# The down product of a mixture-of-experts layer, turned: weights loaded in 32-column pieces for four column groups, token rows streamed, 32x32 block transposes after it

## The chip, the cores and the metric

The kernel runs on one core of a Trainium2 chip. The metric is the device time of one execution in microseconds; the kernel before takes 1264.74 us, the median of three runs.

## What is computed

One inference step of a two-layer decoder: layer 0 mixes tokens by latent attention, layer 1 by causal pooling, and each layer ends in the same kind of mixture of experts. 520 tokens (512 of a prompt, 8 samples) of width 1024 go to 2 of 16 experts each. The part that the change touches is the last line of this function:

```python
def moe(x, w_router, router_bias, w_gate, w_up, w_down):
    B, S, D = x.shape
    t = x.reshape(B * S, D)
    combine = route(t, w_router, router_bias).astype(x.dtype)
    h = jax.nn.silu(jnp.einsum('td,edf->tef', t, w_gate)) * jnp.einsum('td,edf->tef', t, w_up)
    y = jnp.einsum('tef,efd->td', h * combine[:, :, None], w_down)
    return y.reshape(B, S, D)
```

All data are float32. Per expert w_gate and w_up are 1024 x 512, w_down is 512 x 1024: three matrices of 2 MiB.

## The kernel before

All engines run hand-written streams that meet at semaphores. Router and tables sort the tokens by expert into the DRAM tensor `expert_rows` (`xs`), in tiles of `CAP` = 96 rows; a tile belongs to one expert. Here each layer has 16 tiles, so `nh` = 8 passes over a pair of tiles, s = 0 and 1. The result rows of a tile go to the DRAM tensor `expert_out` (`yd`); after the layer's last tile GpSimd (POOL) gathers each token's two rows from there by indirect DMA (L1012) and VectorE (DVE) adds them up with their weights.

A tile (`tl` = 2u + s) goes like this.

- **Weights.** SyncE (SP) issues one DMA for each of the three matrices (`load_expert`, L443, L447, L451) into one of two rings in SBUF. A matrix is loaded for the tile after the next as soon as TensorE is through with it in this tile: the DMAs wait for `gate_ps`, `up_ps` and `down_ps`.
- **Rows in.** ScalarE (ACT) issues four DMAs for the 96 token rows (`load_rows`, L1147), each into 32 partitions, 3 rows of 256 floats to a partition. This is done two tiles ahead, and the four DMAs stand in ACT's stream right behind the store of the tile before. DVE turns the rows with a 32x32 block transpose (`turn_rows`, L1586) into `xeT`, which holds the model width on partitions. In DVE's stream this transpose for the next tile stands between the gate product and the `h` products of this one.
- **Gate, up.** TensorE (PE) multiplies in two column groups (64 weight columns each, `at` = 0 and 64, so that two matmuls share the array), 128 matmuls of 96 streamed columns for each of gate (L851) and up (L861).
- **h.** ACT applies Silu to the gate (L1171), DVE multiplies with up (L1599 for the first three blocks of 128, L1602 for the last) into `h`, which has the expert width on partitions and the 96 rows along the free dimension.
- **Down.** PE takes `h` (128 x 96) as the weights and streams w_down, 512 columns at a time: 16 matmuls (L873) into PSUM banks 4 and 5, one result row to a partition.
- **Rows out.** ACT copies bank 4 (L1175) and DVE bank 5 (L1606) into `ys`; ACT then issues one DMA of 96 rows of 4 KB (L1177). Before writing `ys[s]` both wait for its earlier store (`y_st`).

ACT's stream for a tile is thus: issue the rows of tile tl + 2, Silu, copy bank 4, issue the store. SP's queue and ACT's queue are separate DMA queues that use the same 16 DMA engines.

The prediction names also: `h_set` (DVE tells PE that a part of h is there), `y_set` (banks copied out), `xe_ld` (rows landed), and L1627, DVE's first large step after the last tile of layer 0, which waits for `state_pool`. That is loaded by SP behind the first weights of layer 1.

Of the kernel before, what the change touches and what calls it, by code (L numbers as in the profile page):

```python
# [8 lines left out]
D = 1024  # L9
# [5 lines left out]
KD = D // P  # L15
# [8 lines left out]
KF = F // P  # L24
# [98 lines left out]
def build(nc, t, consts_shape, place):  # L123

    ctx = ExitStack()
    with ctx:
# [104 lines left out]
        ys = [view(arena, 5120 + 1024 * s, D) for s in range(2)]  # L231
# [135 lines left out]
        def _(sp):  # L367
# [87 lines left out]
            for L in range(2):  # L455
# [4 lines left out]
                else:  # L460
                    load_expert(1, 0, 1, (S[0]["gate_ps"][0], nh), (S[0]["up_ps"][0], 2 * nh), (S[0]["down_ps"][0], nh))
# [10 lines left out]
                    load_expert(1, 1, 0, (S[0]["gate_ps"][1], nh), (S[0]["up_ps"][1], 2 * nh), (S[0]["down_ps"][1], nh))  # L472
                sp.wait_ge(tab_set, 2 * L + 2)
                nh = sp.value_load(n_half[0:1, 0:1], min_val=E // 2, max_val=TILES // 2)
                with sp.Fori(1, nh) as u:
                    for s in range(2):
                        ex = sp.value_load(tile_ids[0:1, bass.ds(2 * u + s, 1)], min_val=0, max_val=E - 1)
                        load_expert(L, ex, 1 - s, (q["gate_ps"][s], u), (q["up_ps"][s], 2 * u), (q["down_ps"][s], u))
# [10 lines left out]
        def _(pe):  # L489
# [349 lines left out]
            def experts(L):  # L839
                q = S[L]  # L840

                def tile(u, s):
# [25 lines left out]
                    for blocks in (range(KF - 1), (KF - 1,)):  # L868
                        if KF - 1 in blocks:
                            pe.wait_ge(q["h_set"], 2 * tl + 2)  # L870
                        for hf in range(2):
                            for f in blocks:
                                last = nc.tensor.matmul(bank(4 + hf)[0:CAP, :], h[s][:, f, :], wd[w][:, f, 512 * hf:512 * (hf + 1)],  # L873
                                                        start=(f == 0), stop=(f == KF - 1))
                    last.then_inc(q["down_ps"][s], 1)
# [53 lines left out]
        def _(pool_e):  # L929
# [54 lines left out]
            for L in range(2):  # L984
# [19 lines left out]
                for s in range(2):  # L1004
                    hold(pool_e, q["y_st"][s], 16 * nh)
# [25 lines left out]
        def _(act):  # L1031
# [109 lines left out]
            def experts(L):  # L1141
# [13 lines left out]
                act.sem_inc(q["y_set"], 1)  # L1155

# [7 lines left out]
                def tile(u, s, stored):  # L1164
# [14 lines left out]
                tile(0, 0, False)  # L1179
                tile(0, 1, False)  # L1180
                with act.Fori(1, nh) as u:
                    tile(u, 0, True)
# [497 lines left out]
```

## Time and profile before

| | us |
|---|---|
| median of 3 runs (1263.69 to 1266.37) | 1264.74 |
| the profiled execution | 1262.56 |
| its span, first to last instruction | 1260.8 |
| PE busy, of the span | 1068.2 (85%) |
| DVE busy | 378.2 (30%) |
| ACT busy | 200.1 (16%) |
| expert stage of layer 0, first gate to last down product | 500.3 to 786.3 |
| expert stage of layer 1 | 915.9 to 1201.8 |

The span falls into the attention layer (to 500), 16 tiles, the pooling layer with its router (786 to 916), 16 tiles, and the last normalisation. PE is busy in the profile's sense whenever a matmul is in flight, which doesn't say that it runs at its peak. The granted clock is a share of PE's full clock: 1.00 is 2.4 GHz, 0.50 is 1.2 GHz. The DMA share is the mean busy share of the 16 DMA engines; records can overlap, so it can stand a little above 1.

### The profile page before, as it was taken

To read this page: it belongs to the slowest core of one execution; us is meant where nothing else is said; L and a number is where in the kernel's file an instruction comes from. 1 tells how busy PE (TensorE), PEld (TensorE's weight loads), DVE (VectorE), ACT (ScalarE), POOL (GpSimd) and SP (SyncE) were. 2 spreads that over 40 slices of the span, in tenths; PEclk is the share of its full clock that TensorE was granted. 3 is DMA by queue.
4 is the path that set the end of the run, shared out by engine and by line. 5 is a ranking of instruction groups with operands and counts; after the bars stand their busy time and mean duration, and the time that the engine had idled before them with its cause. 6 is when DMAs were issued, how large, how long until landed. Compare 5 with 4: busy or idle time off the path is not lost.

```text
span 1260.8 us, 27022 instructions
## 1 busy us (share of the span) xinstructions
PE 1068.2 (85%) x11219; PEld 763.1 (61%) x11219; DVE 378.2 (30%) x792; ACT 200.1 (16%) x433; POOL 122.4 (10%) x189
## 2 busy tenths in 40 slices
PE   7899999899999961999999999198099999999910
PEld 6678878545544411777777776187077777777700
DVE  1334444233233233111111111694421111111155
ACT  1234444300222101000000000121020000000011
POOL 0001011120033003000000000430300000000042
PEclk9989999999799975999999999587599999999965
DMA  9324245110023186999999999424479999999541
GB/s 341 138 73 149 80 144 185 56 48 1 1 75 90 53 354 232 325 380 392 392 390 389 399 396 354 157 70 168 151 250 390 384 387 392 402 394 390 202 163 52
DMA packets 80859, 295.96 MB, mean 235 GB/s; under 512 B 10184, under 2 KB 41168, under 8 KB 72495
## 3 DMA queue, kind: packets, MB, share of 16 engines
q1 hardware_dynamic: 53351, 247.50, 52.5%
q10 hardware_dynamic: 19712, 26.75, 6.2%
q0 software_dynamic: 7760, 21.24, 5.1%
q8 instruction: 22, 0.36, 0.1%
q14 instruction: 14, 0.11, 0.0%
HBM read 255.80 MB, written 40.11 MB: 235 GB/s over the span
## 4 chain that ended last, share of the span: by engine, by line
PE 83%; DVE 7%; DMA 3%; POOL 2%; issue 2%; ACT 2%; ACTq 0%; SPq 0%; POOLq 0%; DVEq 0%
PE PS L873 18%; PE PS L851 14%; PE PS L861 13%; PE PS L781 6%; PE PS L569 4%; PE PS L730 4%; PE PS L631 3%; PE PS L616 3%; PE PS L753 2%; PE PS L711 2%; PE PS L786 2%; PE PS L525 2%; PE PS L827 2%; PE PS L547 2%; POOL expert_rows L992 1%
## 5 line engine op out<-in xcount | busy, mean ns | idle before, releaser
L873 PE MATMUL PS<-ring,arena 128*96 128x512 f32 x512 | 227.4, 597 | 0.0
L851 PE MATMUL PS<-arena,ring 128*64 128x96 f32 x4096 | 179.3, 249 | 51.7 <-DVE arena L1586 51.7
L851 PEld LDWEIGHTS PS<-arena,ring 128*64 128x64 f32 x4096 | 173.3, 139 | 75.7 <-issue 75.7
L861 PE MATMUL PS<-arena,ring 128*64 128x96 f32 x4096 | 174.7, 246 | 0.2 <-issue 0.2
L861 PEld LDWEIGHTS PS<-arena,ring 128*64 128x64 f32 x4096 | 171.0, 137 | 0.4 <-issue 0.4
L873 PEld LDWEIGHTS PS<-ring,arena 128*96 128x96 f32 x512 | 80.8, 163 | 123.0 <-issue 119.2
L1586 DVE STREAM_TRANSPOSE arena<-arena 128x768 uint32<-128x768 uint32 x34 | 54.2, 1593 | 205.4 <-ACT arena L1171 175.5
L1606 DVE COPY arena<-PS 96x512 f32<-96x512 f32 x32 | 22.0, 687 | 218.0 <-PE PS L873 218.0
L1175 ACT ACTIVATE arena<-PS 96x512 f32<-96x512 f32 x32 | 19.0, 593 | 379.8 <-PE PS L873 379.8
L1012 POOL DMA_INDIRECT arena<-expert_out,ids x20 | 20.2, 1012 | 599.0 <-DMA expert_out<-arena 589.0
L781 PE MATMUL PS<-ring,arena 128*128 128x512 f32 (+1 forms) x160 | 75.8, 636 | 1.3 <-issue 0.7
L781 PEld LDWEIGHTS PS<-ring,arena 128*128 128x128 f32 (+1 forms) x160 | 28.4, 179 | 45.7 <-issue 45.0
L958 POOL DMA_DIRECT2D ring<-cache_krope x64 | 34.6, 541 | 152.4 <-issue 152.4
L569 PE MATMUL PS<-arena,ring 128*128 128x260 f32 x192 | 47.6, 400 | 1.0 <-POOL ring L936 0.7
L730 PE MATMUL PS<-ring,arena 128*16 128x512 f32 x96 | 44.7, 617 | 2.3 <-ACT arena L1193 2.1
L631 PE MATMUL PS<-ring 128*128 (+1 forms) x320 | 43.4, 271 | 2.0 <-ACT ring L1083 1.6
L800 PE MATMUL PS<-C,X 128*128 128x128 f32 x64 | 17.0, 386 | 31.3 <-POOL X L970 31.3
L631 PEld LDWEIGHTS PS<-ring 128*128 128x128 f32 x320 | 40.1, 191 | 4.6 <-issue 2.3
L569 PEld LDWEIGHTS PS<-arena,ring 128*128 128x128 f32 x192 | 36.9, 199 | 6.6 <-POOL ring L936 0.9
L616 PE MATMUL PS<-ring 128*128 128x512 f32 (+3 forms) x128 | 38.3, 442 | 2.2 <-ACT ring L1070 1.2
L1171 ACT ACTIVATE arena<-PS 128x384 f32<-128x384 f32 x32 | 15.7, 491 | 149.8 <-PE PS L851 149.8
L1078 ACT ACTIVATE ring<-PS,small 128x512 f32<-128x512 f32 (+1 forms) x64 | 33.0, 527 | 25.2 <-DVE small L1330 25.2
(225 smaller groups left out, 1059.7 us busy)
## 6 DMA issues: line engine op xcount, KB each, us to landing
ring<-w_gate SPq DMA_DIRECT2D x32, 2048.0 KB, 14.6
ring<-w_up SPq DMA_DIRECT2D x32, 2048.0 KB, 15.3
ring<-w_down SPq DMA_DIRECT2D x32, 2048.0 KB, 15.7
arena<-expert_rows ACTq DMA_DIRECT2D x144, 96.0 KB, 9.7
expert_out<-arena ACTq DMA_DIRECT2D x32, 384.0 KB, 7.8
expert_rows<-ring SPq DMA_DIRECT2D x6, 1920.0 KB, 10.0
ring<-cache_ckv SPq DMA_DIRECT2D x64, 128.0 KB, 2.0
ring<-w_o SPq DMA_DIRECT2D x1, 4096.0 KB, 19.1
```

What stands on the lines that cost most here:

```text
L525: last = nc.tensor.matmul(bank(n % 4, HALF), wdq[:, k, P * m:P * (m + 1)], XT[:, k, HALF * hf:HALF * (hf + 1)], start=(k == 0), stop=(k == ...
L569: last = nc.tensor.matmul(bank(b, HALF), wuq[:, m, P * parity:P * (parity + 1)], cq[:, m, HALF * hf:HALF * (hf + 1)], start=(m == 0), stop ...
L616: nc.tensor.matmul(score(i), qT[par][:, P * i:P * (i + 1)], kT[par][:, 0:P * (i + 1)], start=True, stop=True).then_inc(s_ps, 1)
L631: last = nc.tensor.matmul(bank(3, 4, VH, off=256 * par)[:, i, :], probT[:, i % 2, P * k:P * (k + 1)], V[:, k, bass.ds(P * p + VH * par, VH ...
L730: nc.tensor.matmul(bank(hf)[0:H, :], qb[s][:, c, :], kpT[:, c, 512 * hf:512 * (hf + 1)], start=(c == 0), stop=(c == 2))
L781: last = nc.tensor.matmul(bank(b0 + hf)[0:n, :], oT[:, k, P * i:P * i + n], wo[:, k, 512 * hf:512 * (hf + 1)], start=(k == 0), stop=(k == ...
L851: last = nc.tensor.matmul(bank(s, KF, CAP)[at:at + 64, f, :], wg[w][:, k, P * f + at:P * f + at + 64], xeT[s][:, k, :], start=(k == 0), st ...
L861: last = nc.tensor.matmul(out[at:at + 64, :], wu[w][:, k, P * f + at:P * f + at + 64], xeT[s][:, k, :], start=(k == 0), stop=(k == KD - 1))
L873: last = nc.tensor.matmul(bank(4 + hf)[0:CAP, :], h[s][:, f, :], wd[w][:, f, 512 * hf:512 * (hf + 1)], start=(f == 0), stop=(f == KF - 1))
L958: pool_e.dma_start(krp[s][:, n, 0, :], t["cache_krope"][0, bass.ds(page, 1), :, :].rearrange("a p d -> (a p) d")).then_inc(kr_ld, 16)
L1078: nc.scalar.activation(prob[:, i, 0:P * (i + 1)], score(i), ACT.Exp, scale=-1.0, bias=mneg[:, c:c + 1], accum_out=rsum[:, c:c + 1]).then_i ...
L1586: v.transpose(xeT[s].rearrange("p m (a j) -> p a m j", j=32).bitcast(mybir.dt.uint32), xe[s].rearrange("p a (i m) -> p a m i", i=32).bitca ...
```

## The change

The down product changes sides. w_down is now the loaded operand: 32 neighbouring columns for each of four column groups, which take columns 256c + 32m for c = 0 to 3; `h` is streamed, 96 columns. That makes 8 x 4 x 4 = 128 matmuls for a tile in place of 16. The result stands turned, output columns on partitions: DVE puts it back with two 32x32 block transposes out of PSUM, which replace both copies. `ys` then has the layout of `xe`, 32 partitions for each quarter of the width, and the store becomes four DMAs with pieces of 256 floats (1 KB). ACT has no copy left. `down_ps` counts twice a tile, `y_st` to 64.

```diff
-        ys = [view(arena, 5120 + 1024 * s, D) for s in range(2)]
+        ys = [view(arena, 5120 + 1024 * s, CAP // 32, D // 4) for s in range(2)]
...
-                        load_expert(L, ex, 1 - s, (q["gate_ps"][s], u), (q["up_ps"][s], 2 * u), (q["down_ps"][s], u))
+                        load_expert(L, ex, 1 - s, (q["gate_ps"][s], u), (q["up_ps"][s], 2 * u), (q["down_ps"][s], 2 * u))
...
-                    for blocks in (range(KF - 1), (KF - 1,)):
-                        if KF - 1 in blocks:
-                            pe.wait_ge(q["h_set"], 2 * tl + 2)
-                        for hf in range(2):
-                            for f in blocks:
-                                last = nc.tensor.matmul(bank(4 + hf)[0:CAP, :], h[s][:, f, :], wd[w][:, f, 512 * hf:512 * (hf + 1)],
-                                                        start=(f == 0), stop=(f == KF - 1))
-                    last.then_inc(q["down_ps"][s], 1)
+
+                    def down(m, blocks):
+                        for f in blocks:
+                            for c in range(4):
+                                last = nc.tensor.matmul(bank(4 + m // 4, 4, CAP)[32 * c:32 * c + 32, m % 4, :],
+                                                        wd[w][:, f, 256 * c + 32 * m:256 * c + 32 * m + 32],
+                                                        h[s][:, f, :], start=(f == 0), stop=(f == KF - 1))
+                        return last
+
+                    down(0, range(KF - 1))
+                    down(4, range(KF - 1))
+                    pe.wait_ge(q["h_set"], 2 * tl + 2)
+                    down(0, (KF - 1,))
+                    down(4, (KF - 1,))
+                    for m in (1, 2, 3, 5, 6, 7):
+                        last = down(m, range(KF))
+                        if m in (3, 7):
+                            last.then_inc(q["down_ps"][s], 1)
...
-                    act.wait_ge(q["down_ps"][s], u + 1)
-                    if stored:
-                        act.wait_ge(q["y_st"][s], 16 * u)
-                    nc.scalar.activation(ys[s][0:CAP, 0:512], bank(4)[0:CAP, :], ACT.Copy).then_inc(q["y_set"], 1)
                     act.wait_ge(q["y_set"], 2 * tl + 4)
-                    act.dma_start(yd[bass.ds(CAP * tl, CAP), :], ys[s][0:CAP, :]).then_inc(q["y_st"][s], 16)
...
+                    for c in range(4):
+                        act.dma_start(yd[bass.ds(CAP * tl, CAP), 256 * c:256 * (c + 1)].rearrange("(a j) d -> j a d", j=32),
+                                      ys[s][32 * c:32 * (c + 1), :, :]).then_inc(q["y_st"][s], 16)
...
-                    dve.wait_ge(q["down_ps"][s], u + 1)
                     if stored:
-                        dve.wait_ge(q["y_st"][s], 16 * u)
-                    v.tensor_copy(ys[s][0:CAP, 512:D], bank(5)[0:CAP, :]).then_inc(q["y_set"], 1)
+                        dve.wait_ge(q["y_st"][s], 64 * u)
+                    for g in range(2):
+                        dve.wait_ge(q["down_ps"][s], 2 * u + g + 1)
+                        v.transpose(ys[s].rearrange("p a (m i) -> p a m i", m=KD)[:, :, 4 * g:4 * g + 4, :].bitcast(mybir.dt.uint32),
+                                    bank(4 + g, 4, CAP).rearrange("p m (a j) -> p a m j", j=32).bitcast(mybir.dt.uint32)
+                                    ).then_inc(q["y_set"], 1)
```

In ACT's stream, one tile of the loop over pairs, before (from the rows-in DMAs on; ISA rows compute an address or wait):

```order
L1147 DMA arena<-expert_rows 32x3x256
L1170 REGISTER_ALU
L1171 ACTIVATE arena<-PS 128x384 [waits gate_ps0_0]
L1174 REGISTER_ALU [waits down_ps0_0]
L1175 ACTIVATE arena<-PS 96x512 [waits y_st0_0]
L1176 ISA
L1177 ISA [waits y_set_0]
L1177 DMA expert_out<-arena 96x1024
L1147 ISA [waits xeT_set_0]
L1147 DMA arena<-expert_rows 32x3x256
```

The same piece of ACT's stream now:

```order
L1157 DMA arena<-expert_rows 32x3x256
L1178 REGISTER_ALU
L1179 ACT_TABLE_LOAD
L1179 ACTIVATE arena<-PS 128x384 [waits gate_ps0_0]
L1180 ISA
L1182 ISA [waits y_set_0]
L1182 DMA expert_out<-arena 32x3x256
L1182 ISA
L1182 DMA expert_out<-arena 32x3x256
L1182 ISA
L1182 DMA expert_out<-arena 32x3x256
L1182 ISA
L1182 DMA expert_out<-arena 32x3x256
```

The copy and its waits are gone; four DMAs with the shape of the rows-in DMAs stand where one stood, ahead of the next tile's rows. A load of the activation table stands in the loop, ahead of the wait for the gate product.

In DVE's stream, one tile of the loop, now:

```order
L1600 ISA [waits sg_set_0]
L1590 STREAM_TRANSPOSE arena<-arena 128x3x8x32 [waits xe_ld1_0]
L1603 TENSOR_TENSOR arena<-arena,PS 128x288 [waits up_ps0_0]
L1605 REGISTER_ALU
L1606 TENSOR_TENSOR arena<-arena,PS 128x96 [waits up_ps0_0]
L1608 REGISTER_ALU
L1611 STREAM_TRANSPOSE arena<-PS 128x3x128 [waits down_ps0_0,y_st0_0]
L1611 STREAM_TRANSPOSE arena<-PS 128x3x128 [waits down_ps0_0]
```

The order of the steps is as before; the two transposes out of PSUM stand where the copy of bank 5 stood. The turn of the next tile's rows still stands ahead of both h products.

## Rows read from the trace of the kernel before

**Rows 1.** The page's part 5: line, engine, operation, shapes, count; busy us, mean ns.
```profile
L873 PE MATMUL PS<-ring,arena 128*96 128x512 f32 x512 | 227.4, 597 | 0.0
...
L1586 DVE STREAM_TRANSPOSE arena<-arena 128x768 uint32<-128x768 uint32 x34 | 54.2, 1593 | 205.4 <-ACT arena L1171 175.5
```

**Rows 2.** The chain that ended last, one tile of layer 0: start us, us.
```profile
619.55 7.04 PE PS L873 x16
626.59 5.43 PE PS L851 x128
632.02 5.28 PE PS L861 x128
```

**Rows 3.** The same chain, layer 1: its first gate product, last down product, last store.
```profile
915.89 7.35 PE PS L851 x128
...
1194.74 7.05 PE PS L873 x16
1202.68 3.04 DMA expert_out<-arena
```

**Rows 4.** A window in layer 0's tiles: busy by engine, granted clock, DMA share, GB/s.
```profile
572.00:750.00 178.00, 178.00 (x2723) 131.41 (x2722) 29.93 (x40) 10.85 (x20) 0.00 (x0) 1.00 1.02 392
```

**Rows 5.** Loads of w_down issued from 500 to 540 us: issue to landing.
```profile
DMA to landing us min/median/max: 12.2/12.6/12.9
```

**Rows 6.** Loads of w_down issued from 1120 to 1170 us: issue to landing.
```profile
DMA to landing us min/median/max: 16.4/16.5/16.5
```

**Rows 7.** Timeline of SP's DMA issues, the last of layer 1.
```profile
1166.32 0.38 SPq L451 DMA_DIRECT2D ring<-w_down  x1
```

**Rows 8.** The page's part 3: SP's queue (q1), ACT's (q10): packets, MB, share.
```profile
q1 hardware_dynamic: 53351, 247.50, 52.5%
q10 hardware_dynamic: 19712, 26.75, 6.2%
```

**Rows 9.** The page's part 6: ACT's two kinds of DMA: count, KB each, us to landing.
```profile
arena<-expert_rows ACTq DMA_DIRECT2D x144, 96.0 KB, 9.7
expert_out<-arena ACTq DMA_DIRECT2D x32, 384.0 KB, 7.8
```

**Rows 10.** Timeline of ACT, 655 to 692 us, behind the down product ending at 662.1.
```profile
663.08 0.36 ACTq L1177 DMA_DIRECT2D expert_out<-arena  x1
663.63 1.77 ACTq L1147 DMA_DIRECT2D arena<-expert_rows  x4
```

**Rows 11.** Loads of expert_rows issued from 640 to 700 us: issue to landing.
```profile
DMA to landing us min/median/max: 8.4/10.1/12.1
```

**Rows 12.** Timeline of DVE, 655 to 692 us.
```profile
662.22 0.69 DVE L1606 COPY arena<-PS 96x512 f32<-96x512 f32 x1 [6.87 <-PE PS L873]
...
672.85 0.26 DVE L1602 TENSOR_TENSOR arena<-arena,PS 128x96 f32<-128x96 f32 x1 [0.87 <-PE PS L861]
...
685.93 1.59 DVE L1586 STREAM_TRANSPOSE arena<-arena 128x768 uint32<-128x768 uint32 x1 [5.38 <-ACT arena L1171]
```

**Rows 13.** Timeline around the router's last part, layer 0: PE and its weight loads.
```profile
465.37 1.02 PE L503 MATMUL PS<-C,X 8*128 8x8 f32 x8 [5.64 <-DVE X L1453]
...
466.67 0.47 PEld L827 LDWEIGHTS PS<-wr,ring 128*8 128x8 f32 x16 [0.38 <-ACT ring L1121]
466.67 0.59 PE L827 MATMUL PS<-wr,ring 128*8 128x16 f32 x16 [0.29 <-ACT ring L1121]
```

**Rows 14.** The window around it; columns as in rows 4.
```profile
465.00:470.00 5.00, 1.61 (x24) 1.40 (x24) 2.01 (x8) 1.92 (x4) 0.00 (x0) 0.50 1.01 429
```

**Rows 15.** Windows of 3 us within one tile; columns as in rows 4.
```profile
663.90:666.90 3.00, 3.00 (x78) 3.00 (x76) 0.00 (x0) 0.00 (x0) 0.00 (x0) 1.00 1.02 434
...
669.80:672.80 3.00, 3.00 (x75) 2.88 (x70) 0.46 (x1) 0.00 (x0) 0.00 (x0) 1.00 1.05 342
```

**Rows 16.** Timeline behind layer 0's last tile, whose down product ended at 786.3 us.
```profile
787.76 1.28 ACT L1126 ACT_TABLE_LOAD   x1 [0.80 <-DVE arena L1606]
...
790.88 2.29 DVE L1627 TENSOR_TENSOR arena<-arena 128x2048 f32<-128x2048 f32 x1 [3.69 <-DMA arena<-state_pool]
```

More of the change, by code:

```diff
@@ L460, in _ @@
                 else:
-                    load_expert(1, 0, 1, (S[0]["gate_ps"][0], nh), (S[0]["up_ps"][0], 2 * nh), (S[0]["down_ps"][0], nh))
+                    load_expert(1, 0, 1, (S[0]["gate_ps"][0], nh), (S[0]["up_ps"][0], 2 * nh), (S[0]["down_ps"][0], 2 * nh))
                     sp.wait_ge(S[0]["xeT_set"], 2 * nh + 1)
@@ L470, in _ @@
                     sp.dma_start(t["o_pool_s"][0, :, CTX - 1, :], X[0:DB, 4, :]).then_inc(pool_out, 16)
-                    load_expert(1, 1, 0, (S[0]["gate_ps"][1], nh), (S[0]["up_ps"][1], 2 * nh), (S[0]["down_ps"][1], nh))
+                    load_expert(1, 1, 0, (S[0]["gate_ps"][1], nh), (S[0]["up_ps"][1], 2 * nh), (S[0]["down_ps"][1], 2 * nh))
                 sp.wait_ge(tab_set, 2 * L + 2)
@@ L1004, in _ @@
                 for s in range(2):
-                    hold(pool_e, q["y_st"][s], 16 * nh)
+                    hold(pool_e, q["y_st"][s], 64 * nh)
                 def gather(i):
@@ L1154, in experts @@
                 nh = act.value_load(n_half[0:1, 0:1], min_val=E // 2, max_val=TILES // 2)
-                act.sem_inc(q["y_set"], 1)
                 act.wait_ge(scat, 160 * (L + 1))
@@ L1162, in experts, with tile @@
                     nc.scalar.activation(X[0:n, i, :], X[0:n, i, :], ACT.Copy, scale=ALPHA).then_inc(xscaled, 1)
-                def tile(u, s, stored):
+                def tile(u, s):
                     tl = 2 * u + s
@@ L1171, in tile @@
                     nc.scalar.activation(sg[s], bank(s, KF, CAP), ACT.Silu).then_inc(q["sg_set"], 1)
-                    act.wait_ge(q["down_ps"][s], u + 1)
-                    if stored:
-                        act.wait_ge(q["y_st"][s], 16 * u)
-                    nc.scalar.activation(ys[s][0:CAP, 0:512], bank(4)[0:CAP, :], ACT.Copy).then_inc(q["y_set"], 1)
                     act.wait_ge(q["y_set"], 2 * tl + 4)
-                    act.dma_start(yd[bass.ds(CAP * tl, CAP), :], ys[s][0:CAP, :]).then_inc(q["y_st"][s], 16)
[L1179 to L1182, printed above, removed]
-                    tile(u, 1, True)
+                    for c in range(4):
+                        act.dma_start(yd[bass.ds(CAP * tl, CAP), 256 * c:256 * (c + 1)].rearrange("(a j) d -> j a d", j=32),
+                                      ys[s][32 * c:32 * (c + 1), :, :]).then_inc(q["y_st"][s], 16)
+                with act.Fori(0, nh) as u:
+                    tile(u, 0)
+                    tile(u, 1)
             def take_pages(b):
@@ L1582, in experts @@
                 nh = dve.value_load(n_half[0:1, 0:1], min_val=E // 2, max_val=TILES // 2)
-                dve.sem_inc(q["y_set"], 1)
+                dve.sem_inc(q["y_set"], 2)
                 def turn_rows(s):
```

## The prediction

> **What bounds the kernel now.** I read the chain of waits first. In an expert stage it is TensorE alone: a tile takes 7.04 us of down product, 5.43 of gate and 5.28 of up [rows 2], 17.75 us from one down product to the next, 16 tiles in each of two layers, 32 in all. PE waits for nothing between tiles. Seen from PE alone, every microsecond off the down product is worth 32.
>
> The DMA view says otherwise. While PE sets the pace, the DMA engines' share is 1.02 at 392 GB/s [rows 4]. A tile needs three matrices of 2,097,152 bytes, four row loads of 98,304 and a store of 393,216, in all 7.08 MB, and 7.08 MB at 392 GB/s is 18.0 us, a bit more than the 17.75 that PE gives. That the loads fall behind shows in their landing: w_down takes 12.6 us early in layer 0 [rows 5] and 16.5 late in layer 1 [rows 6]. PE doesn't notice, for two whole tiles are in the rings when a stage begins. So the kernel is bound by PE, with the DMA engines full right behind it.
>
> The third view is ACT's queue. It has 19,712 packets [rows 8]. Its 144 row loads and 32 stores [rows 9] are 176 DMAs; with 96 pieces and 16 completions each that is 176 x 112 = 19,712, so completions count as packets. A tile's row loads and store are 5 x 112 = 560 packets. SP's matrices have 128, 128 and 512 pieces (16 KB, 16 KB, 4 KB) and 48 completions: 816. The store is issued at 663.08 and the four row loads up to 665.4 [rows 10]; the last has landed by 665.4 + 12.1 = 677.5 [rows 11]. ACT's 560 packets thus took 14.4 us at most, 39 or more per us; SP's 816 in 17.75 us are 46 per us. The counts per time are alike, though SP's packets are many times larger. I read this as **turns**: a DMA engine takes one packet from each queue in turn, whatever its size. The Trainium skill, DMA: Bandwidth & Descriptors, section Queues, rings and completion order, says that each engine goes round robin over the queues at packet granularity; it speaks of several descriptors to a packet, which no row here shows.
>
> **Down product.** 16 matmuls of 597 ns (they overlap, so that 16 take 7.04 us) [rows 1, 2] go; 128 with 32 columns loaded and 96 streamed come. No row has this form. From one side: the gate and up products stream the same 96 columns, 128 matmuls in 5.28 us, 41.3 ns each and 82.5 for a pair of column groups. If four groups fit in the time of two, a matmul costs 20.6 ns and a tile 2.6 us. From the other: if there is no more overlap than now, 41.3 ns and 5.3 us. Narrow weights are issued fast: 16 loads of 8 columns in 0.47 us, 29 ns each [rows 13], at a granted clock of 0.50 [rows 14]. I take 27 ns, near that row: **3.4 us**. PE's tile is then 5.43 + 5.28 + 3.4 = 14.1 us. The second wait for h is covered: DVE begins L1602 as up ends and takes 0.26 us [rows 12], and 24 matmuls at 27 ns stand ahead of the wait, 0.65 us. The rule of the Trainium skill that speaks against the change is in TensorE: Matmul & The Clock Gate, section Wait — 56ns, not 53.3ns?: about 62 ns per matmul where the sequencer decodes in software, 7.9 us for 128, which would make this product dearer than before. The 41.3 ns of rows 2 disagree with it; its other floor, 25 ns, would give 3.2 us.
>
> **Copies.** ACT's 0.59 us copy goes. DVE's goes too (0.69), and two transposes of 128 x 384 come. L1586 takes 1.59 us for 128 x 768 [rows 1], so I put 0.80 on each; reading PSUM might add a little. The first lies beside the down product, the second is exposed only before the store: +0.1 us. DVE is 30% busy. ACT's table load is now in the loop, 8 times a layer, 1.28 us each [rows 16]. It stands ahead of the wait for the gate product: after the store and row issues ACT is free about 5.5 us into the gate product of 5.4, so Silu comes late by half a us at worst, and L1599 still waits for up.
>
> **Store.** One DMA of 4 KB pieces becomes four of 1 KB pieces. Issue: three more at 0.36 us [rows 10], +1.1. Bytes are the same. Engine time: ACT's queue used 6.2% of 16 engines for 26.75 MB, 46.8 us per MB; SP's 42.8 [rows 8]. If only the row loads are dearer (14.16 MB), they cost 50.3, and the store at that price is 7.5 x 0.393 / 16 = +0.18 us a tile. That is the lower bound, and I take it. The upper: while row loads and w_down are in flight the rate falls from 434 to 342 GB/s [rows 15]; if the store does that for another 6 us, it costs 21% of 6, +1.25 us a tile. Nothing argues for a gain.
>
> **Turns.** This is the costly part. The store has 4 x 112 packets, ACT's queue 896 a tile, SP's still 816. Turn by turn, 896 take 896/46 = **19.5 us**, longer than PE's 14.1 and than the 18.0 of the bytes. Who waits: the rows of tile n+3 stand behind the store of tile n. They are there at most 15.4 us after n's down product ended at 662.1 [rows 10 to 12], and are turned at 685.9, 23.8 us after, one period and 6.1. Now they come 1.2 us later (issue) and 336/46 = 7.3 us later (turns): 23.9. Needed they are after 14.1 + 6.1 = 20.2 us while PE runs free, after 18.0 + 6.1 = 24.1 if the bytes bound. So they are late as soon as PE has sped up, and since each tile adds 1.5 us to the queue, they stay late. DVE stands at L1586 for them, with both h products behind it, and PE waits between up and down, 19.5 - 14.1 = 5.4 us. After an idle of 5.64 us the clock row shows 0.50, that is 1.2 GHz [rows 13, 14], and a first gate product after idle took 7.35 for 5.43 [rows 3]; I put nothing on these 1.9 us since PE has 5.4 to spare.
>
> **Sum, per layer.** Tiles 0 to 2 have their rows early and the last waits for none: 4 x (14.1 - 17.75) = -14.6. Twelve at 19.5: +21.0. SP's loads meanwhile run ahead (18.0 against 19.5, after three fast tiles); when both rings are full its queue empties, ACT's pieces go without taking turns, and a tile runs at 14.1. I count one such: -5.4. Net +1.0. The end: second transpose and issue, +1.2. Two layers: 2 x 2.2 = +4.4. The profiled execution, 1262.56 (span 1260.8), becomes 1267.0; it lies 2.2 below the median shown, and against that I say **1269.1**. With none or two such tiles per layer: 1280 or 1258.
>
> **Rivals.**
> A, ends faster: turns don't bind, rows arrive in time, the bytes bound the stage. w_down of the last tile is issued at 1166.32 [rows 7] and lands 16.5 later, 1182.8; the loads are full from early on, so it can't come much sooner. Add 14 x 0.18 = 2.6 and a down product of 3.4: 1188.8 against 1194.74 + 7.05 = 1201.8, -13.0 per layer. Ends +2.4; behind layer 0 `state_pool` (now used 4.6 us after the last product [rows 16]) queues behind more of layer 1's weights, +4.5. Sum -26.0 + 6.9 = -19.1: **1246**, give or take 6. For it: the 24.1 against 23.9 above; it decides if the queue takes under 18.0 us for its packets, that is 50 per us. Against: rows 10 and 11.
> B: the store disturbs the loads by 1.25 us a tile, 28 tiles: +35, **1304**. For it the dip [rows 15]; against, the dip needs writes into 32 partitions, and a store reads there.
> C: four groups don't overlap at all, 82.5 x 128 = 10.6 us; 3.5 x 32 = +113, **1378**. It decides from 55 ns a matmul (7.04/128). Against: two groups overlap now.
> D: the DMA engines have room (the rate is only what PE asks) and rows come in time: -3.65 x 32 = -117, plus 2.4 for the ends, **1150**. Against: the landings that grow.
>
> **Chances.** Forecast 0.60, A 0.26, B 0.08, C 0.03, D 0.03. 0.2% is 2.5 us, about what can be told from no change here. Of the forecast's 0.60, which spreads over 1258 to 1280, 0.13 lies faster, 0.12 within, 0.35 slower. Faster: 0.13 + 0.26 + 0.03 = 0.42; same 0.12; slower 0.35 + 0.08 + 0.03 = 0.46. The range takes in most of A and the first part of B's price: 1243 to 1287; D, C and most of B are left out. The forecast's own is 1258 to 1280.
>
> **What would show it.** Right: the down product in 2.6 to 5.3 us; idle time before it, or before h, put down to row loads; row loads landing 20 us and more after issue, up from 10; ACT's queue at 272 x 112 = 30,464 packets; dips of the granted clock inside the stages; a few tiles near 14 us, the others over 18. Wrong: row loads landing within 18 us and PE waiting for the ring's loads instead (A); a down product over 7 us (C); matrices landing later and later with rows in time (B); no waits at all (D).

## The result, and the profile after

The changed kernel takes **1494.21 us** (median of 4 runs, 1483.13 to 1498.01), against 1265.55 for the kernel before (1263.69 to 1272.49): ratio 1.178, 95% interval 1.170 to 1.186. The prediction was 1269.1, from 1243 to 1287. The sign is the likelier one (slower had 0.46), the size is wrong: 229 us more, where the forecast had 4, and none of the cases had the cause.

The page after, the lines that answer to rows 1, 8 and 9:

```profile
span 1496.3 us, 42722 instructions
...
PE 1101.0 (74%) x18899; PEld 919.4 (61%) x18899; DVE 393.6 (26%) x824; ACT 199.0 (13%) x415; POOL 121.5 (8%) x189
...
q1 hardware_dynamic: 53351, 247.50, 45.7%
q10 hardware_dynamic: 30464, 26.76, 6.1%
...
q8 instruction: 162, 2.65, 0.7%
...
L851 PE MATMUL PS<-arena,ring 128*64 128x96 f32 x4096 | 226.5, 281 | 145.3 <-issue 93.3
...
L872 PE MATMUL PS<-arena,ring 128*32 128x96 f32 x8192 | 207.9, 261 | 104.4 <-issue 104.4
...
L1611 DVE STREAM_TRANSPOSE arena<-PS 128x384 uint32<-128x384 uint32 x64 | 37.3, 583 | 283.4 <-PE PS L872 283.4
...
arena<-expert_rows ACTq DMA_DIRECT2D x144, 96.0 KB, 5.9
```

The same two lines of the page before:

```profile
q8 instruction: 22, 0.36, 0.1%
...
L851 PE MATMUL PS<-arena,ring 128*64 128x96 f32 x4096 | 179.3, 249 | 51.7 <-DVE arena L1586 51.7
```

Three things stand out. PE now has idle time put down to **issue**: it waited for no other engine and no transfer that the profile can name. Queue q8, which brings instructions, has 162 packets where it had 22. And the row loads, which the prediction saw as the late ones, land in 5.9 us, sooner than before [rows 9]. The waits of PE, with total, times and longest:

```profile
PE PS L872 <- issue: 104.4, 51, 3.9
PE PS L851 <- issue: 93.3, 29, 5.2
PE PS L851 <- DVE arena L1590: 52.0, 2, 26.1
PE PS L861 <- issue: 5.1, 5, 1.3
```

The 52.0 are the start of the two stages and were there before. The other three make 203 us, new. The chain that ended last shows where they lie; two tiles of layer 0, to be held against rows 2:

```profile
596.93 3.45 issue
600.38 7.40 PE PS L851 x128
607.78 5.28 PE PS L861 x128
613.07 2.61 PE PS L872 x119
615.67 1.41 issue
617.08 2.84 PE PS L872 x128
619.92 2.26 issue
622.19 0.41 PE PS L872 x9
622.59 5.43 PE PS L851 x128
628.02 5.28 PE PS L861 x128
633.30 2.60 PE PS L872 x117
635.90 3.70 issue
639.60 5.35 PE PS L872 x128
644.95 0.03 issue
644.97 0.66 PE PS L872 x11
645.63 3.43 issue
649.07 7.02 PE PS L851 x127
```

PE stops **every 128 matmuls** (a few less where waits and register instructions stand between them). Each matmul record comes with a weight load (8192 of each for L872), so 128 matmuls are 256 instruction records. q8 moved 2.65 MB in 162 packets, 16.4 KB each, so one packet is 64 bytes for each of 256 records. The 140 packets more are 8.75 for each of the 16 passes of the loop, and a pass has 2048 records (2 tiles of 512 matmuls and 512 loads) besides waits and registers, 8 packets' worth. I read this so, and the runs below test it: after each block of 256 records PE has nothing to issue until the next block has come, and the whole body is brought anew in every pass. In the gate and up products 128 matmuls last 5.3 us and the gap is mostly covered; in the down product they last 2.6 to 2.8 and it is not.

The blocks don't lie alike in the two layers. In layer 0 seven stops stand at the gate product, one for each backward branch (23.1 us). In layer 1 there are 22: seven at the branch, seven more 13 matmuls behind it, the rest in the pass's second tile. One of layer 1's passes, right behind the branch:

```profile
1123.43 1.38 PE PS L851 x13
1124.81 4.33 issue
```

Near the end of layer 1, when the last weights have landed (DMA share 0.03 from 1414.6 to 1420.0), the whole down product of 256 matmuls runs without a stop:

```profile
1414.59 5.45 PE PS L872 x256
```

The second part is the clock, in windows of the same stretch (columns as in rows 4):

```profile
600.00:604.00 4.00, 3.62 (x46) 3.62 (x48) 0.00 (x0) 1.28 (x1) 0.00 (x0) 0.50 1.03 386
...
622.00:628.00 6.00, 5.81 (x141) 5.67 (x142) 0.58 (x1) 0.00 (x0) 0.00 (x0) 1.00 0.70 231
...
640.00:645.00 5.00, 4.97 (x128) 4.62 (x120) 0.58 (x1) 0.00 (x0) 0.00 (x0) 0.50 0.54 225
```

After an idle of 3.45 or 3.70 us the granted clock is 0.50 (1.2 GHz), and 128 matmuls of the down product take 5.35 us for 2.84; after 2.26 us it is still 1.00. These two tiles take 649.07 - 600.38 = 48.7 us, before 35.5. Of the 13.2 more, issue is 10.8, the low clock 5.8 (the products' 37.9 against 2 x (5.43 + 5.28 + 5.34) = 32.1; the 256 matmuls of a down product at full clock take the 5.34 that 128 of them take at 0.50), and the cheaper down product gives back 3.4. Over the layers, first gate to last down product: 386.7 us (502.5 to 889.2) and 418.7 (1018.2 to 1437.0), against 286.0 and 285.9. That is 233.5 of the 235.5 us between the spans.

The loop over 320 us of layer 0 (560 to 880):

```profile
560.00:880.00 320.00, 246.74 (x6766) 236.30 (x6762) 47.11 (x67) 14.08 (x19) 0.00 (x0) 0.89 0.80 291
```

The DMA engines are no longer full (0.80 for 1.02 [rows 4]), so neither turns nor bytes can be what binds here.

### The profile page after: what moved, and what is told of

Its sections match the earlier page's. It is cut to its first block, busy times and chain, and to the rows that moved or that the text cites. A ratio compares the mean times of both kernels' runs of the same rounds, so it can differ in the third digit from the quotient of the medians.

```text
span 1496.3 us, 42722 instructions
## 1 busy us (share of the span) xinstructions
PE 1101.0 (74%) x18899; PEld 919.4 (61%) x18899; DVE 393.6 (26%) x824; ACT 199.0 (13%) x415; POOL 121.5 (8%) x189
## 3 DMA queue, kind: packets, MB, share of 16 engines
q10 hardware_dynamic: 30464, 26.76, 6.1%
q8 instruction: 162, 2.65, 0.7%
## 4 chain that ended last, share of the span: by engine, by line
PE 72%; issue 15%; DVE 6%; DMA 3%; POOL 2%; ACT 2%; ACTq 0%; SPq 0%; POOLq 0%; DVEq 0%
PE PS L851 15%; PE PS L872 14%; PE PS L861 11%; PE PS L781 5%; PE PS L569 3%; PE PS L730 3%; PE PS L631 3%; PE PS L616 2%; PE PS L753 2%; PE PS L525 2%; PE PS L711 2%; PE PS L786 1%; PE PS L827 1%; PE PS L547 1%; POOL expert_rows L1002 1%
## 5 line engine op out<-in xcount | busy, mean ns | idle before, releaser
L851 PE MATMUL PS<-arena,ring 128*64 128x96 f32 x4096 | 226.5, 281 | 145.3 <-issue 93.3
L851 PEld LDWEIGHTS PS<-arena,ring 128*64 128x64 f32 x4096 | 218.1, 164 | 154.2 <-issue 152.3
L872 PE MATMUL PS<-arena,ring 128*32 128x96 f32 x8192 | 207.9, 261 | 104.4 <-issue 104.4
L872 PEld LDWEIGHTS PS<-arena,ring 128*32 128x32 f32 x8192 | 189.8, 117 | 118.7 <-issue 115.0
L861 PE MATMUL PS<-arena,ring 128*64 128x96 f32 x4096 | 178.4, 246 | 5.2 <-issue 5.1
L861 PEld LDWEIGHTS PS<-arena,ring 128*64 128x64 f32 x4096 | 173.3, 137 | 6.9 <-issue 6.5
L1611 DVE STREAM_TRANSPOSE arena<-PS 128x384 uint32<-128x384 uint32 x64 | 37.3, 583 | 283.4 <-PE PS L872 283.4
```

The source lines that it names most:

```text
L851: last = nc.tensor.matmul(bank(s, KF, CAP)[at:at + 64, f, :], wg[w][:, k, P * f + at:P * f + at + 64], xeT[s][:, k, :], start=(k == 0), st ...
L861: last = nc.tensor.matmul(out[at:at + 64, :], wu[w][:, k, P * f + at:P * f + at + 64], xeT[s][:, k, :], start=(k == 0), stop=(k == KD - 1))
L872: last = nc.tensor.matmul(bank(4 + m // 4, 4, CAP)[32 * c:32 * c + 32, m % 4, :], wd[w][:, f, 256 * c + 32 * m:256 * c + 32 * m + 32], h[s ...
L1611: v.transpose(ys[s].rearrange("p a (m i) -> p a m i", m=KD)[:, :, 4 * g:4 * g + 4, :].bitcast(mybir.dt.uint32), bank(4 + g, 4, CAP).rearra ...
```

## The experiments

Theory F (fetch): the loop body of PE has outgrown what stays loaded, and the dense down product uses up instructions faster than they come. Rivals: the form with four column groups is slow in itself; the store's small pieces (turns, as predicted); a backward branch alone. The kernel before, run beside them, had medians of 1264.7 (runs 1 to 4), 1262.0 (5 to 8) and 1263.6 (9 to 12). Edits are against the changed kernel unless said otherwise; of the longer ones only the lines that carry the change are shown, and they shift the line numbers, so that the down product stands at L872, L873 or L874. Runs 4 to 8 and run 12 have one execution each, the others 4 to 10.

**1. Two column groups** instead of four: half the instructions for the same result. The columns are taken 8 apart, and DVE's transposes write them 8 apart too. Body 1536 records.

```diff
+                        n = 4 if False else 2
...
-                            for c in range(4):
-                                last = nc.tensor.matmul(bank(4 + m // 4, 4, CAP)[32 * c:32 * c + 32, m % 4, :],
-                                                        wd[w][:, f, 256 * c + 32 * m:256 * c + 32 * m + 32],
...
+                            for c in range(n):
+                                cols = wd[w][:, f, D // n * c:D // n * (c + 1)].rearrange("p (i m) -> p i m", m=KD)[:, :, m]
+                                last = nc.tensor.matmul(bank(4 + m // 4, 4, CAP)[P // n * c:P // n * (c + 1), m % 4, :],
```

> The changed kernel, but with two column groups of 64 in place of four of 32 (columns 8i + m of a half, which the second transpose puts back): 64 matmuls of the program a tile for the down product, not 128, and a PE loop body of 1536 matmul and load records in place of 2048. Theory F (the loop body is larger than what TensorE's sequencer keeps, so its code is loaded anew in every pass, behind the weights in the DMA queues): the instruction queue falls from 162 packets to about 22 as before, the idle time put down to issue inside the expert stages goes, the down product stays near 5.3 us, and the time is 1225 to 1275 us. Rival G (four column groups or the turned form are slow in themselves, by drains between forms): the drains stay, since gate, up and down are still turned products, and the time stays above 1350. Rival T (ACT's queue with 896 packets a tile bounds the stage): row loads land late and DVE waits for them, 19.5 us a tile, 1265 to 1320 us.

Measured: **1284.6** us, ratio 1.014 (1.009 to 1.019). q8 has 25 packets, and of the issue waits in the tiles 0.2 us is left. 209.6 us are gone, and still the time lies over the 1225 to 1275 that theory F had. Besides the number of instructions and of groups only the order of the columns is new, and run 4 takes that by itself. What is left over the kernel before is something else: 64 columns that lie 8 apart load slowly (218 ns a load; 140 dense, L851), and the down product takes 7.76 us, more than the 7.04 it replaced.

```profile
L874 PEld LDWEIGHTS PS<-arena,ring 128*64 128x64 f32 x4096 | 252.5, 218 | 3.9 <-issue 3.9
```

**2. The kernel before, with four tiles instead of two in a pass** (against the kernel before). Every instruction is the same; body 2176 records.

```diff
-                with pe.Fori(0, nh) as u:
-                    for s in range(2):
-                        tile(u, s)
+                with pe.Fori(0, E // 4) as v4:
+                    for d in range(2):
+                        for s in range(2):
+                            tile(2 * v4 + d, s)
```

> The kernel before, with four tiles in place of two in a pass of TensorE's loop (and a fixed number of passes): the same matmuls in the same order, but a body of 2176 records where it had 1088. Theory F: code is loaded again in each of the 8 passes, about 9 packets each, so the instruction queue goes from 22 packets to about 90, and there is idle time put down to issue; since the down product of 512 columns gives 7 us for few records, much of it can be hidden: 10 to 80 us slower. Rivals G and T: no change, within 3 us of the kernel before.

Measured: **1291.0** us, ratio 1.020 (1.015 to 1.025), q8 90 packets. The waits appear without any turned product:

```profile
PE PS L851 <- issue: 11.5, 12, 2.6
PE PS L861 <- issue: 8.3, 8, 1.5
```

They are 20 us and not 200. There are half as many blocks (38 packets in each stage, against 71 and 78 in the change), and the 16 long matmuls of a down product last 7 us for 32 records, in which I take it that the next block comes.

**3. The kernel before with only its store split** into four DMAs of 1 KB pieces (against the kernel before): the prediction's turns by themselves.

```diff
-                    act.dma_start(yd[bass.ds(CAP * tl, CAP), :], ys[s][0:CAP, :]).then_inc(q["y_st"][s], 16)
+                    for c in range(4):
+                        act.dma_start(yd[bass.ds(CAP * tl, CAP), 256 * c:256 * (c + 1)], ys[s][0:CAP, 256 * c:256 * (c + 1)]
+                                      ).then_inc(q["y_st"][s], 16)
```

> The kernel before, with the store of a tile's result as four DMAs of 96 pieces of 1 KB in place of one with 96 of 4 KB: ACT's queue has 896 packets a tile in place of 560, nothing else is changed. Theory T: 896 packets at 46 per us take 19.5 us where a tile has 17.75; row loads land some 7 us later, and after a few tiles DVE waits for them: 10 to 50 us slower. Theory F alone: no change, row loads later but in time, within 5 us.

Measured: **1277.8** us, ratio 1.010 (1.006 to 1.013). Row loads land in 18.7 us instead of 9.7, DVE waits for them, and PE from there for h (16 waits, 16.1 us in all):

```profile
DVE arena L1588 <- DMA arena<-expert_rows: 240.9, 28, 15.2
```

A stage takes 294.4 and 295.4 us, 18.4 a tile. The waits are there as forecast, for +13 us; it can't be what costs 229.

**4. Four groups, columns 8 apart**: the stride of run 1 in the form of the change.

```diff
+                        n = 4 if True else 2
...
-                                                        wd[w][:, f, 256 * c + 32 * m:256 * c + 32 * m + 32],
...
+                                cols = wd[w][:, f, D // n * c:D // n * (c + 1)].rearrange("p (i m) -> p i m", m=KD)[:, :, m]
```

> The changed kernel with four column groups as it is, but the same column order as in the run with two groups (columns 8i + m of each quarter, read with a stride of 32 bytes): the control for the stride. Theory F: as the changed kernel, about 160 instruction packets and 1470 to 1510 us, if a strided load of 32 columns costs what a dense one does. If the stride makes the loads dearer, the down product's busy time grows beyond 5.4 us a tile and the time with it.

Measured: 1495.6 us, q8 162, issue waits 99.2 + 95.3 + 7.1. The stride lengthens a load of 32 columns (143 ns for 117) and costs no time beside the stops. So runs 5, 6 and 12, which mix both group counts and need it, can be read against the change.

**5, 6 and 12. Smaller bodies**, by taking the first of the eight m with four groups and the rest with two, with the columns 8 apart as in runs 1 and 4:

```diff
+                        n = 4 if m < 5 else 2
-                            for c in range(4):
+                            for c in range(n):
```

(m < 7 gives 1984 records, m < 5 gives 1856, m < 2 gives 1664.)

> Four column groups for seven of the eight column positions m and two groups for the last: 120 down matmuls of the program a tile in place of 128, so TensorE's loop body has 1984 matmul and load records, 3% fewer than the 2048 of the changed kernel, and otherwise the same work. Theory F, code is kept if the whole body fits in 2048 records: the instruction queue falls to about 25 packets and the time to 1250 to 1290 us. If the limit is in whole blocks of 256 records and the body lies across nine of them: still about 160 packets and 1450 to 1500 us. If the number of records doesn't matter but the form of four groups does: 1450 us or more with few packets.

> As the run before, with four groups for five of the eight positions and two for three: a body of 1856 records, 7.25 blocks of 256. Theory F: it lies across eight or nine blocks; about 25 packets and 1255 to 1295 us if eight are kept, about 160 packets and over 1400 us if it happens to touch nine. Down product about 5 x 0.67 + 3 x 0.97 = 6.2 us a tile.

> Four column groups for m = 0 and 1, two for the rest (strided columns as in the run with two groups): body of PE's loop 1664 records, between 1536 (q8 25, no issue waits, 1284.6) and 1856 (q8 154, 137 us of issue waits, 1441.5). If a loop is kept only up to some size that lies between 1664 and 1856, q8 stays near 25 and the time is near 1284. If the limit lies between 1536 and 1664, q8 is near 130 packets (6.5 of 256 records a pass, 16 passes, and the 22 of the rest) and issue waits come back, of some 100 us: 1380 to 1420. A middle case, q8 around 50 and waits of 20 us, would say that the kept part shrinks gradually.

| body, records | q8 packets | issue waits in the tiles, us | time, us |
|---|---|---|---|
| 2048 (the change) | 162 | 203 | 1494.2 |
| 1984 | 162 | 190 | 1514.6 |
| 1856 | 154 | 137 | 1441.5 |
| 1664 | 26 | 2 | 1298.5 |
| 1536 (run 1) | 25 | 0.2 | 1284.6 |

It is a **step, and it lies between 1664 and 1856 records**. At 1664 the mix of both forms of matmul runs without a gap:

```profile
602.92 5.28 PE PS L861 x128
608.20 8.19 PE PS L874 x160
616.38 5.28 PE PS L851 x128
```

So four groups don't leave gaps by themselves; and that they aren't slow in themselves the change's own chain says, with 119 of its matmuls in 2.61 us. Above the step q8 has no middle value: everything is fetched in each pass, not only what doesn't fit (at 1856 each stage of 8 passes has 70 packets). The 14 us between 1664 and 1536 are the down product's 8.19 us for 7.76. At 1984 the waits are a little fewer, yet the time is 20 us longer, and over the 1450 to 1500 expected for a body across nine blocks; its two-group part loads slowly, and I leave the rest open.

**7. PE's loop unrolled**, so that no branch goes back.

```diff
-                with pe.Fori(0, nh) as u:
+                for u in range(E // 2):
```

> The changed kernel with TensorE's loop over the 8 pairs written out as straight code, so that no branch goes back. Theory F, with code arriving about every 5 us a block of 256 records behind the weight traffic: the records used are the same, 64 blocks a layer, so it stalls about as much, 1400 to 1500 us, with 150 or more packets. Rival, the backward branch is what defeats the fetching ahead: 1250 to 1320 us with as many packets.

Measured: **1421.5** us, q8 141.

```profile
PE PS L872 <- issue: 139.0, 59, 3.9
PE PS L851 <- issue: 7.4, 3, 3.1
```

Of the 93 us of waits at the gate product 86 are gone, but not all of them were the branch's. In the change the 14 stops right at the branch make 46.6 us (one is the 3.43 at 645.63), those 13 matmuls behind it, in layer 1, another 31.5, and 15.3 stand in the second tile of a pass, where only a block ends. The waits inside the down product stay, and grow by 35. In all 149.5 of 203 us are left: straight code streams too slowly as well, and that is the greater part.

The Trainium skill, Runtime: NRT & Kernel Launch, section Instruction fetch mechanics, describes blocks of 16 KiB or 256 instructions, and a stall after a taken branch whose target is outside a window of two pages. The size agrees with the packets here (16.4 KB, 128 matmuls apart). The stops at the branch agree with the stall, but the window does not: the kernel before goes back over 1088 records, more than four blocks, and has no such stop. The Trainium skill also says, in the same section, that crossing a block is mostly hidden, because an engine issues more slowly than blocks arrive. Here PE issued 256 records in 2.6 to 2.8 us, and the trace disagrees, with gaps of 1.4 to 3.9 us. And the Trainium skill gives PE, in the same section, room for 2048 instructions. That is eight blocks, and the runs leave it open: at 1856 records a pass has 8.75 packets, since waits and registers come on top of the records and a loop need not begin where a block does.

**8. Less weight traffic.** From a layer's third tile on, the loads bring an eighth of w_gate and w_up and a quarter of w_down; PE's instructions are all there, and it multiplies with what older weights stand in the ring for the rest. The DMA share in the tiles falls to 0.38 and 0.33.

```diff
-                sp.dma_start(wg[s], t["w_gate"][L, bass.ds(e, 1), :, :].rearrange("a (p k) f -> p (a k) f", p=P)
+                sp.dma_start(wg[s][:, 0:n, :], t["w_gate"][L, bass.ds(e, 1), :, :].rearrange("a (p k) f -> p (a k) f", p=P)[:, 0:n, :]
```

> The changed kernel with only an eighth of each gate and up matrix and a quarter of each down matrix loaded from the third tile of a layer on; the rest of a matrix is what stood in the ring, so the outputs are not the reference's. TensorE's program is the same, 160 instruction packets. Theory F, a code packet waits behind weight packets in the 16 DMA engines: the waits put down to issue shrink from 203 us to under 80 and the time to 1200 to 1350 us. Rival, the fetch takes its time by itself whatever else the DMA engines do: the waits stay near 200 us and the time near 1490 us.

Measured: 1335.5 us, q8 162 as in the change.

```profile
PE PS L852 <- issue: 66.3, 29, 3.7
PE PS L873 <- issue: 13.4, 18, 2.8
```

(L852 is the gate and L873 the down product here.) The same blocks come over the same DMA engines. With these a third busy, the stalls inside the down product shrink from 104 us to 13. Of the 93 at the gate product 66 stay, and they divide: the 14 stops at the branch take 48.3 us for 46.6, those 13 matmuls behind it 14.2 for 31.5, the others 3.8 for 15.3. So a block of instructions **waits behind the weights**, and that is most of what PE loses in straight code; the stop at the branch itself, 3.3 to 3.5 us, doesn't shrink with the traffic.

**9. Two groups of 64 neighbouring columns** (512c + 64m), so that loads are dense. The result's columns then stand in another order, and the two sums at the end take them by halves.

```diff
+                            for c in range(2):
+                                last = nc.tensor.matmul(bank(4 + m // 4, 4, CAP)[64 * c:64 * c + 64, m % 4, :],
+                                                        wd[w][:, f, 512 * c + 64 * m:512 * c + 64 * m + 64],
```

> The turned product with two column groups of 64 neighbouring columns each (columns 512c + 64m), so that weights are loaded dense; the columns of a row of expert_out stand in another order, and the last step's sums undo that with halves. Body of PE's loop: 1536 records. Fetch theory: q8 stays near 25 packets, no issue waits in the loop, granted clock as before; the down product costs what a gate product costs, 5.3 us a tile, PE's tile 16.0. Then the ACT queue's 896 packets a tile (18.3 to 18.5 us a tile in the run with the split store alone) or the bytes (18.0) set the stage: 1258 to 1280. If the strided loads were all that cost in the first two-group run (7.8 against 5.3 us, while PE had no idle time to give), it should come out below that run's 1284.6. If it is 1290 or more, something other than fetch and stride is slow in the turned product. If it is under 1240, neither turns nor bytes bind.

Measured: **1273.9** us, ratio 1.009 (1.006 to 1.012). The down product takes 5.28 us at full clock, but PE isn't what sets the pace; it waits for h 23 times, 51.2 us in all. The down products of the chain begin at 633.73 and 672.07 with row loads ahead of them:

```profile
DVE arena L1597 <- DMA arena<-expert_rows: 283.3, 28, 15.3
```

A stage takes 293.7 and 290.9 us, the pace of run 3 (18.4 a tile) or a little under it, though run 3's down product was the old one. PE has become faster by 1.8 us a tile and next to none of it arrives.

**10. The same with the stores issued from POOL's queue**, so that ACT's queue has only the rows.

```diff
+                        hold(pool_e, q["y_set"], 2 * tl + 4)
+                        for c in range(4):
+                            pool_e.dma_start(yd[bass.ds(CAP * tl, CAP), 512 * (c % 2) + 256 * (c // 2):512 * (c % 2) + 256 * (c // 2) + 256].rearrange("(a j) d -> j a d", j=32),
+                                             ys[s][32 * c:32 * (c + 1), :, :]).then_inc(q["y_st"][s], 16)
```

> As e9, but the four store DMAs of a tile are issued from POOL's queue, so that ACT's queue has the row loads alone (448 packets a tile) and the stores take turns of their own. Turns theory (a queue with more packets a tile than SP's 816 sets the pace): row loads land in about 10 us again and the stage goes at the bytes' 17.8 to 18.0 a tile, some 10 to 15 us under e9: about 1250, with 1240 to 1262 as limits. If the bytes or PE bound e9, nothing changes (within 4 us of e9). If the small store pieces disturb the weight loads wherever they are issued from, it is not faster than e9 either, and w_down lands later than 17 us.

Measured: **1257.1** us, ratio 0.9948 (0.9927 to 0.9969): faster than the kernel before, by half a per cent. Median landings, run 9 and then this run:

```profile
ring<-w_down SPq DMA_DIRECT2D x32, 2048.0 KB, 13.2
arena<-expert_rows ACTq DMA_DIRECT2D x144, 96.0 KB, 20.1
```

```profile
ring<-w_down SPq DMA_DIRECT2D x32, 2048.0 KB, 26.0
arena<-expert_rows ACTq DMA_DIRECT2D x144, 96.0 KB, 9.8
```

Two things differ, the queue of the stores (POOL's is q0, software_dynamic in the page) and, with it, the place of the rows: ACT no longer waits for `y_set` ahead of them, and issues them 8 us before the down product ends (612.08 for 620.0), where run 9 does it 3 us after (608.60 for 605.5). Run 11 has this early place with the stores still in ACT's queue. The rows land after half the time, the weights 13 us later, and PE now waits for weights, a little at a time (15.5 us for w_down, 11.1 for w_up). The stage takes 277.1 and 277.6 us, 17.3 a tile, but that is a mean of two paces. In each stage five or six tiles in a row go at 15.8, which is PE alone (three times 5.28). The last six go at 18.5:

```profile
682.15 5.50 PE L872 MATMUL PS<-arena,ring 128*64 128x96 f32 x128 [1.28 <-DMA ring<-w_down]
700.65 5.50 PE L872 MATMUL PS<-arena,ring 128*64 128x96 f32 x128 [0.90 <-DMA ring<-w_down]
```

Run 9's tiles go at 18.5 (layer 1: 18.4) from the second on, and in both runs the DMA engines are full; windows of run 9 and run 10, columns as in rows 4:

```profile
560.00:760.00 200.00, 181.38 (x4207) 179.92 (x4209) 34.97 (x55) 13.10 (x17) 0.00 (x0) 0.97 1.02 382
560.00:760.00 200.00, 188.41 (x4486) 185.49 (x4484) 40.43 (x58) 13.59 (x18) 24.66 (x46) 1.00 1.02 387
```

So the queue doesn't change what the DMA engines get done, it changes **who waits**. In run 9 the rows are late while weights lie ready (they land after 13.2 us); in run 10 PE first uses up the two tiles of weights in the rings at its own pace, and then takes the pace of the DMA engines. That is where the 13 to 17 us a stage come from. Between the stages 5.5 us are lost again (135.1 for 129.6), where `state_pool` takes 25.3 us.

**11. As run 9, the rows issued right behind Silu**, ahead of the store.

```diff
-                    act.wait_ge(q["xeT_set"], tl + 1)
-                    load_rows(s, bass.ds(CAP * (tl + 2), CAP))
...
+                    act.wait_ge(q["xeT_set"], tl + 2)
+                    load_rows(1 - s, bass.ds(CAP * (tl + 3), CAP))
                     act.wait_ge(q["y_set"], 2 * tl + 4)
```

> As e9, but ACT issues the row loads of tile tl + 3 right behind Silu, ahead of the store of tile tl and not behind it; number and size of DMAs are the same. If what e9 loses to turns is only the place of the rows behind the store, rows land earlier than they are needed and DVE's wait for them goes: 1245 to 1260. If ACT's queue is too long for a tile altogether (896 packets), the order changes nothing: within 4 us of e9. No issue waits and q8 near 25 by the fetch theory.

Measured: 1268.0 us, ratio 1.003 (1.0005 to 1.005), between what the two readings had said. The chain now runs through the stores (39.5% of it from 600 to 680 us in `expert_out<-arena`), so the same queue is late with something else. A stage takes 286.6 and 286.4 us, 17.9 a tile, and it has one tile's rows more to load in each layer. Of the 17 us between runs 9 and 10 the place alone is thus worth 6, and the queue of the stores, with the place the same, the other 11.

## Why the prediction was wrong

**The step that failed is the one under "Down product": "I take 27 ns ... 3.4 us".** It failed twice.

First, a miscount. I wrote 128 matmuls, from the loops 8 x 4 x 4. The profile has 256 records a tile, 8192 over 32. The sign was in the rows: the old down product is 2 halves x 4 blocks = 8 matmuls in its code and x16 in rows 2. Each float32 matmul stands there twice, with two loads. A record takes 20.9 ns, right at the 20.6 I had as the lower bound: 128 take 5.35 us at half the clock, at 639.60, and all 256 take 5.45 in one piece at 1414.59. But 256 of them are 5.3 us: the upper of the two bounds. PE's tile is 16.05 us, not 14.1. Case C, no overlap, is excluded: four groups do go together. They don't gain over two, which also take 5.28 (run 9); a group half as wide needs twice the matmuls.

Second, and this is the 229 us: **the sum had no term for the instructions themselves.** I counted for each engine what it does, for each queue its packets, and took it that PE's instructions are simply there. q8 stands in the same part of the page as the two queues I counted, with 22 packets, and the loop's 1088 records went to 2048. The Trainium skill has a warning on branches in the section named above, and I didn't draw on it; it would have pointed to the stops at the branch (46.6 us here), hardly to the 104 to 139 us in straight code.

By the prediction's own steps:

- **Turns (the forecast).** What they were to do, they do in runs 3 and 9: rows land after 18.7 and 20.1 us for 9.7, DVE waits for them and PE for DVE. The pace that I gave them, 19.5 us a tile, is not there and not theirs: run 9 goes at 18.5 with 896 packets a tile in ACT's queue, and run 10, with 448, at the same 18.5 once its rings have no weights ahead. It is the work of the DMA engines as a whole that sets it; which queue a piece stands in decides who waits. That the engines go strictly in turn no run here shows. In the change itself none of this mattered: with PE at 24 us a tile the row loads land in 5.9. "A few tiles near 14 us" didn't occur.
- **The sum without fetch.** Run 9 is the change as I had imagined it, but with two groups: 1273.9, against 1269.1 predicted. It agrees partly by luck: PE's tile was 2 us too short in my sum, which is hidden under the wait for rows, and the pace of the late tiles 1 us too long.
- **A, the bytes.** This is what binds from the middle of a stage when the rows are in time: run 10, 1257.1 against the 1246 of A. Its last down product ends at 1193.1 for 1188.8 in A, and the loss at `state_pool` is 5.5 for 4.5.
- **B, the store disturbs the loads by 1.25 us a tile.** Too much: run 10 has the same pieces, and its DMA-bound tiles take 18.5 us, 0.5 over the 18.0 that I had for the bytes. So the pieces cost at most about 0.5 a tile, more than the 0.18 in the sum.
- **C and D.** C is excluded by the 5.3 us. D is excluded by run 10, where PE waits for weights.
- **Copies.** A transpose out of PSUM takes 0.58 us, not 0.80, and ACT's table load stays hidden: there are 16, and the two tiles of the chain above hold PE and issue alone. ACT's queue has the 30,464 packets.
- **The clock.** I put nothing on it since PE had time to spare. In the change PE had none, and it costs 5.8 us in 48.7.

Layer 1 loses 32 us more than layer 0. Its blocks lie otherwise, with a second stop behind each branch: issue waits are 113.3 us there for 89.6, and the granted clock is 0.85 for 0.89.

What stays open: the exact size of what stays loaded, between 1664 and 1856 records, and whether it counts records or whole blocks; what the stop at the branch consists of; and the extra 20 us at 1984. The change with a single tile in a pass, four groups throughout in 1024 records, was not run; it would show the four groups with no fetch beside them.

## What to carry to other kernels

Count instruction records, as the profile has them and not as the loops do, before splitting work into smaller matmuls: here a loop body went from 1088 to 2048, the queue that brings instructions from 22 packets to 162, and PE stood still every 256 records. Two questions price it: does the body still fit (1664 did, 1856 did not), and how long does PE need for 256 records while the DMA engines are full (5.3 us was mostly covered, 2.7 was not). And when a store is cut into small pieces, look at which queue it shares and what stands behind it: another queue for the stores was worth 11 us here, and 17 with the rows issued earlier; only with that was the turned product, in two groups, faster than the kernel before, by 6.5. A mean over a stage can hide two paces: run 10's 17.3 us a tile is 15.8 and then 18.5.

## What was unexpected of the hardware

- A loop one step too large isn't fetched in part: q8 goes from 26 packets to 154 between 1664 and 1856 records, and the gate product, which the change doesn't touch, is hit too (busy 226.5 us for 179.3, and 93 us of waits).
- Instructions travel over the same DMA engines as the weights, and wait behind them: 104 us of stalls in the down product with the full loads, 13 with small ones. The stop at a backward branch doesn't shrink with it (14 stops, 46.6 us and 48.3).
- Strided weight loads cost by width: 64 columns 8 apart 218 ns for 140, and the product grows from 5.28 to 7.76 us; 32 columns 143 ns for 117, without effect on the change's time (run 4).
- A 32x32 block transpose of 128 x 384 takes 583 ns when it writes runs of 32, and 882 when it writes 8 apart (run 1).
